# A twentieth buffer for weights in a two-block transformer kernel, and ten pairs of buffers from the ninth expert on

## The chip, the core and the metric

The kernel runs as one launch on one core of one Trainium2 chip. The metric is the device time of an execution in microseconds (us). Three runs of the kernel before took 1641.13, 1641.85 and 1643.40 us; their median, 1641.85 us, is the time before. The execution that was profiled took 1642.62 us, and its instructions span 1640.8 us.

## The reference

Two transformer blocks work on 256 tokens of width 1024, all in float32. The first has a mixer (sliding-window attention beside gated linear attention) and then a mixture of 32 experts, of which each token takes four. The second is a dense block with two feed-forward layers around another mixer. What matters here is the mixture:

```python
logits = (h @ w_router) + b_router
top_v, top_i = lax.top_k(logits, 4); gates = jax.nn.softmax(top_v, axis=-1)
...
u = xb @ w_mlp1[e] + b_mlp1[e]                 # w_mlp1[e]: 1024 x 2048, 8 MB
a = x_glu * jax.nn.sigmoid(1.702 * x_glu) * (x_lin + 1)   # x_glu, x_lin clipped at 7
y = a @ w_mlp2[e] + b_mlp2[e]                  # w_mlp2[e]: 1024 x 1024, 4 MB
out = zeros.at[slot_tok].add(y * gate)
x = x + gt2 * rms_norm(out, g_post_ffn)
```

Every expert's 12 MB are read once, so the mixture reads 384 MB, and the whole program 547 MB.

## The kernel before

**Slots.** Weights go from the chip's memory through buffers of 8192 bytes a partition, 1 MB each, called slots (`SLOT`, `NSLOT = 19`). Slots 0 to 6 (`NEAR = 7`) belong to the weights all the time. Slots 7 to 18 ("far" in the code) lie over tiles of the first mixer, and each may be filled only when its gate (`slot_gate`, L1162 to L1167, L1276 and L1303) is open, which means that the tiles under it have had their last reader. Behind slot 18 begins the region (`moe0`, L234) with `gg2` (the row with which the mixture's output is scaled at its end), `brow`, the split weights `whf`/`wlf` of the mixer, and the small tiles of the mixture.

**Chunks.** I number the 1 MB chunks of the mixture 0 to 383: chunk 12e + j is the j-th of expert e, j = 0 to 7 of `w_mlp1` and 8 to 11 of `w_mlp2`. They are loaded in that order, all by SyncE's queue (SP in the profile), which is one list made at L2119 to L2134: each load waits until the chunk that held its slot has been read for the last time, and a load that waits holds back all behind it. TensorE gives the sign: behind the last matmul of every chunk it raises the semaphore `rel`. I call this the release of the chunk.

**Which slot.** For experts 0 to 8 (`LONE = 9`) every load is one chunk, and the slots follow the list `order` of 19 numbers, again and again (L298 to L301). For experts 9 to 30 one load brings two chunks (2 MB) into a pair of neighbouring slots. The pairs follow `ring` (L303), which has nine of them, starting at slots 7, 9, 11, 13, 15, 17, 1, 3 and 5; slot 0 is not used then. A pair's load waits for the releases of both chunks that lie in its two slots. The list of pairs is cut at its front (L304), so that it ends with the ring's end at expert 30. Expert 31 has single loads again, in slots 7 to 18. The dense block that follows uses slots 0 to 6 alone.

**Experts.** The program has for each expert three ways: for up to 32 tokens (near), up to 64 (middle), and more (far, L1638), and each engine branches by the count. TensorE, VectorE and ScalarE pass the chunk's results on in the usual way: first matmuls with `w_mlp1`, then the gated activation (DVE, ACT), transposes, and second matmuls with `w_mlp2`. Between the first and the second an odd expert also gathers the tokens of the next two experts (`prepare`).

**gg2.** It is written by ScalarE's queue early, before expert 0 (L1713): two loads of 256 KB, each of 128 rows of 2 KB. It is read by `residual` after expert 31 (L1764).

Of the kernel before, what the change touches and what calls it, by code (L numbers as in the profile page):

```python
# [7 lines left out]
F32 = mybir.dt.float32  # L8
F32R = mybir.dt.float32r
# [4 lines left out]
D = 1024  # L14
NE = 32
EPS = 1e-6
SLOT = 8192
NEAR = 7
NSLOT = 19
LONE = 9  # L20
NPIECE = 4
NEG = -1.0e30
FAR = 3.0e38
# [131 lines left out]
def two_block_forward(  # L155
# [31 lines left out]
    with ctx:  # L187
# [7 lines left out]
        end = nc.sbuf_usable_end // 32 * 32  # L195

        place = {}

        class Arena:
# [30 lines left out]
        z0 = near + NEAR * SLOT  # L230
        slots = [
            nc.alloc_sbuf_tensor_at(f"slot{i}", [128, 2048], F32, offset=near + i * SLOT) for i in range(NSLOT)
        ]
        moe0 = near + NSLOT * SLOT  # L234
        both = {
            i: nc.alloc_sbuf_tensor_at(f"slots{i}", [128, 4096], F32, offset=near + i * SLOT)
            for i in [*range(NEAR, NSLOT, 2), 1, 3, 5]
        }


        slot_sem = [sem(f"slot{i}") for i in range(NSLOT)]
        chunks = []
        slot_gate = [[] for _ in range(NSLOT)]

        def chunk(src, slot, width=2048):
            chunks.append({"src": src, "slot": slot, "sem": slot, "w": width, "done": None})
            return len(chunks) - 1

        def two_chunks(src, slot):

            first = chunk(src, slot, 4096)
            chunks.append({"src": None, "slot": slot + 1, "sem": slot, "w": 2048, "done": None})
            return [first, first + 1]
# [42 lines left out]
        c_out = stream(lambda j: w_out[j], 4, slots_=(0, 1, 4, 2))  # L296

        far = lambda *i: [NEAR + j for j in i]  # L298
        order = [3, 5] + far(1) + [6] + far(0) + [0] + far(3, 6, 7) + [1] + far(5, 2) + [4] + far(4) + [2] + far(9, 10, 11, 8)
        assert sorted(order) == list(range(NSLOT))  # L300
        singles = order * NE  # L301
        last_singles = far(*range(12))
        ring = [*range(NEAR, NSLOT, 2), 1, 3, 5]  # L303
        pairs = (ring * NE)[-6 * (NE - 1 - LONE) :]  # L304
        c_w1, c_w2 = [], []
        for e in range(NE):
            if LONE <= e < NE - 1:
                ids = [two_chunks(w[e, j], pairs.pop(0)) for w, n in ((w_mlp1, 4), (w_mlp2, 2)) for j in range(n)]
                ids = [i for two in ids for i in two]
            else:  # L310
                src = [w[e, j // 2][:, j % 2 * 2048 : j % 2 * 2048 + 2048] for w, n in ((w_mlp1, 8), (w_mlp2, 4)) for j in range(n)]
                ids = [chunk(i, singles[12 * e + j] if e < LONE else last_singles[j]) for j, i in enumerate(src)]
            c_w1.append(ids[:8])
# [42 lines left out]
        def load(q, s, dst, src, *after):  # L356
# [35 lines left out]
        bias_ada = [nc.alloc_sbuf_tensor_at("badat0", [128, 512], F32, offset=place["gg"][0]), badat]  # L392
        wl_last = rare("wl_last", [128, 1024], F32R)
# [11 lines left out]
        og = over("og", "att_s0", "att_s0", [128, 2, 512])  # L405
        atth1 = over("atth1", "gq", "gat", [128, 4, 256], F32R)
        attl1 = over("attl1", "gqt", "gkt", [128, 4, 256], F32R)
        later = Arena(moe0, end)
        gg2 = later("gg2", [128, D])
        bias_ada.append(nc.alloc_sbuf_tensor_at("badat2", [128, 512], F32, offset=place["gg2"][0]))  # L410
        brow = later("brow", [128, 1536], F32R)
        rare = Arena(z0 + 10 * SLOT, moe0)
        XH = rare("XH", [128, 8, 256], F32R)
        XL = rare("XL", [128, 8, 256], F32R)
        sq = over("sq", "XH", "XH", [128, D])
        tmp2 = over("tmp2", "XL", "XL", [128, 2, D])
        np_slots = [
            (later(f"whf{i}", [128, 1024], F32R), later(f"wlf{i}", [128, 1024], F32R) if i < NPIECE - 1 else wl_last)
            for i in range(NPIECE)
        ]  # L420
        wrt = later("wrt", [128, 8, NE])
        tri_s = later("tri_s", [128, 128])

# [4 lines left out]
        s_gg, s_gg2 = sem("s_gg"), sem("s_gg2")  # L428
# [74 lines left out]
        pieces = []  # L503
# [52 lines left out]
        T = {}  # L556
# [41 lines left out]
        def rows_in(dst, r0, s_, *after):  # L598
            return [load(act, s_, dst[:, 512 * g : 512 * g + 512], mod_rows[r0 + g : r0 + g + 1, :].to_broadcast([128, 512]),
                         *after) for g in range(2)][-1]  # L600
# [28 lines left out]
        p_out = add_pieces(c_out)  # L629
# [32 lines left out]
        for k in range(8):  # L662
            i = k % 4
            src = bank[2 + i][:, (k // 4) * 256 : (k // 4) * 256 + 256]
            a_, b_ = a1[:, k : k + 1], sh1[:, k : k + 1]
# [495 lines left out]

        for i, gate_ in enumerate((  # L1162
            [T["pv"]], [T["pt1"]], [T["ov"], T["o"]], [T["pv"], T["o"]], [pieces[p_out + 3]["used"]], [t_og], [T["o"], T["r"]],
            [T["o"], T["r"]], [], [], [], [],
        )):
            slot_gate[NEAR + i] = gate_

# [3 lines left out]
        moe = Arena(place["brow"][1], end)  # L1171
# [7 lines left out]
        u_g, u_s, u_l = (moe(n, [128, 512]) for n in ("u_g", "u_s", "u_l"))  # L1179
# [10 lines left out]
        xt_x = moe("xt_x", [128, 8, 32])  # L1190
        at_x = nc.alloc_sbuf_tensor_at("at_x", [128, 4, 64], F32, offset=place["xt_x"][0])
        sel32 = [[moe(f"sel32{i}{j}", [128, 64]) for j in range(2)] for i in range(2)]
        y_x = moe("y_x", [64, D])


        t_tr, t_ns = [[], []], []
# [32 lines left out]
        def selections(p):  # L1229

            i = p % 2
            pool.wait([pe.now()])
            for s_ in range(2):
                e = 2 * p + s_
                one = zsel[:, :].rearrange("p (h e) -> p h e", h=2)[:, :, e : e + 1]
                cp(pool, sel32[i][s_][:, :].rearrange("p (h j) -> p h j", h=2), one.to_broadcast([128, 2, 32]))
                t_selt[i] = cp(pool, selt[i][s_][:, :].rearrange("p (h j) -> p h j", h=2), one.to_broadcast([128, 2, 64]))
# [112 lines left out]
        def prepare(p, half):  # L1350
            i = p % 2
            ks = range(4 * half, 4 * half + 4)
            if p == 0:
                new = gather(oh, xt, t_oh[0], ks=ks, b0=2, at=slice(64, 128))
                t_xt[0] = [t_xt[0][0], (t_xt[0][1] if half else []) + new]
                if half:
                    t_ws[0], _ = weights_t(ow, ws[0], 3, t_ow[0])
                return
            new = gather(oh, xt, t_oh[i], ks=ks)
            t_xt[i] = [t_xt[i][s_] + new for s_ in range(2)] if half else [new, new]  # L1360
            if half:
                t_ws[i], _ = weights_t(ow, ws[i], 1, t_ow[i])
# [347 lines left out]
            q.wait([t_a2, t_sh2])  # L1710
        t_xt[0] = [gather(oh, xt, t_first[0], b0=2, at=slice(0, 64)), []]

        T["gg2"] = rows_in(gg2, 2, s_gg2, T["gg2"])  # L1713
        t_nm = ts(dve, nmax, top8[:, :, 0], -1.0, ALU.mult, t_sl1)
        for b in range(2):
            t_e = af(gate[:, b, :], lg[:, b, :], ACT.Exp, t_nm, bias=nmax[:, b : b + 1])
# [10 lines left out]
        for p in range(NE // 2):  # L1727
            if 0 < p < NE // 2 - 1:
                one_hots(p + 1)
                selections(p + 1)  # L1730
            t_even = expert(2 * p, [lambda b=b: scatter(p - 1, False, [b]) if p else prepare(0, b) for b in range(2)])
            if p == 0:
                one_hots(1)
                selections(1)
            t_odd = expert(2 * p + 1, [lambda h_=h_: prepare(p + 1, h_) for h_ in range(2)] if p + 1 < NE // 2 else [nothing] * 2)
            t_yp[p % 2] = t_even + t_odd
        warm(3, 0)
# [324 lines left out]
        for b in range(2):  # L2062
            for g in range(2):
                c = slice(512 * g, 512 * g + 512)
# [172 lines left out]
```

How the kernel before makes its waits and increments, by code:

```python
    def run(items):  # L69
        for it in items:
            if it[0] == "wait":
                eng.wait_ge(it[1], it[2])
            elif it[0] == "op":
                it[1](eng)
            elif it[0] == "sig":
                it[1](eng).then_inc(it[2], it[3])
            elif it[0] == "step":
                eng.sem_inc(it[1], it[2])
            elif it[0] == "home":
```

## Time and profile before

| what | us |
|---|---|
| median of 3 runs | 1641.85 |
| lowest and highest run | 1641.13, 1643.40 |
| profiled execution | 1642.62 |
| its span | 1640.8 |
| TensorE busy in the span | 1445.6 (88%) |
| VectorE, ScalarE, GpSimd busy | 589.1, 471.4, 123.0 |
| experts 0 to 31, first to last matmul, about | 160 to 1085 |
| dense block after them | 1085 to 1640 |

The profile is of one execution. In its strip of 40 slices a slice is 41 us. "DMA" is the mean busy share of the 16 DMA engines over which each transfer is spread; a transfer has landed when all its parts have, so its landing tells of the last engine. In the views of windows the columns are the window's ends, its length, the busy time of each engine with its count of instructions, the granted clock of TensorE, the DMA share and the rate.

### The profile page before, as it was taken

The page shows a single profiled execution, that of the slowest core. Times are in us where ns is not written, and L with a number is a line of the kernel's source. Part 1 is how long each engine was busy: PE and PEld are TensorE (multiplying, and loading weights), DVE is VectorE, ACT ScalarE, POOL GpSimd, SP SyncE. Part 2 cuts the span into 40 slices and gives each one's busy share as a digit, 9 for nine tenths or more (in the row PEclk, how much of TensorE's full clock was granted, in tenths as well). Part 3 has the DMA queues.
Part 4 walks back from the last instruction along what each step waited for, and adds up shares of the span by engine and source line. Part 5 has one row for each costly group of instructions (what it writes and reads, how often), then busy time and mean ns, then how long its engine had stood idle before and what let it go on. Part 6 is the DMA issues. An engine that isn't in the chain of part 4 may idle for free.

```text
span 1640.8 us, 20608 instructions
## 1 busy us (share of the span) xinstructions
PE 1445.6 (88%) x8414; PEld 842.7 (51%) x8414; DVE 589.1 (36%) x957; ACT 471.4 (29%) x836; POOL 123.0 (7%) x254
## 2 busy tenths in 40 slices
PE   5999988896868787887689788899999999999998
PEld 2767433332322332332233233258888878788886
DVE  3676211220110111221111111156654677665654
ACT  3644201110110110110000101045553674565543
POOL 2001301110110110110110110000000010000000
PEclk9999989998889997999889999999999999999999
DMA  9999999999999999989999999986555443555540
GB/s 384 404 359 361 420 423 425 424 424 429 429 429 428 429 427 429 397 339 430 429 426 428 428 428 428 426 346 224 181 200 184 180 133 124 230 195 203 178 157 26
DMA packets 57944, 547.43 MB, mean 334 GB/s; under 512 B 6548, under 2 KB 6932, under 8 KB 9000
## 3 DMA queue, kind: packets, MB, share of 16 engines
q1 hardware_dynamic: 56736, 542.95, 80.8%
q8 instruction: 107, 1.75, 0.4%
q10 hardware_dynamic: 1032, 2.16, 0.4%
q14 instruction: 69, 0.57, 0.1%
HBM read 544.03 MB, written 1.06 MB: 332 GB/s over the span
## 4 chain that ended last, share of the span: by engine, by line
PE 64%; DMA 25%; issue 4%; DVE 3%; POOL 2%; ACT 1%; POOLq 0%; DVEq 0%; SPq 0%; ACTq 0%
PE bank L330 62%; DMA slots<-w_mlp 20%; DMA slot<-w_mlp 4%; PE bank L334 2%; DMA slot<-w_in_tail 1%; POOL oh L345 1%; POOL ow L345 1%; DVE u_l L348 0%; DVE u_l L345 0%; DVE u_g L344 0%; DVE u_s L340 0%; PE bank L1472 0%; DVE h L348 0%; DVE XL L340 0%; ACT xt L337 0%
## 5 line engine op out<-in xcount | busy, mean ns | idle before, releaser
L330 PE MATMUL bank<-slots,xt 128*32 128x512 f32 (+1 forms) x1408 | 268.6, 702 | 67.2 <-DMA slots<-w_mlp 66.4
L330 PE MATMUL bank<-wht,XH 128*128 128x512 f32 x528 | 207.1, 397 | 4.4 <-DVE wlt L340 2.7
L348 DVE SCALAR_TENSOR_TENSOR wlt<-slot,colt,wht 128x512 fp32r<-128x512 f32 x248 | 177.4, 761 | 79.2 <-ACT wht L337 79.0
L344 DVE TENSOR_SCALAR u_g<-bank 64x512 f32<-64x512 f32 (+1 forms) x34 | 23.3, 686 | 503.3 <-PE bank L330 496.0
L330 PE MATMUL bank<-wht,XL 128*128 128x512 f32 x528 | 203.7, 390 | 0.0
L330 PE MATMUL bank<-wlt,XH 128*128 128x512 f32 x528 | 203.6, 390 | 0.0
L330 PEld LDWEIGHTS bank<-slots,xt 128*32 128x32 f32 (+1 forms) x1408 | 71.6, 135 | 256.2 <-issue 152.4
L337 ACT ACTIVATE wht<-slot,colt 128x512 fp32r<-128x512 f32 x248 | 164.5, 718 | 92.3 <-PE bank L330 92.3
L337 ACT ACTIVATE u_s<-u_g 64x512 f32<-64x512 f32 (+1 forms) x34 | 21.4, 630 | 525.7 <-DVE u_g L344 525.7
L330 PE MATMUL bank<-slots,at 128*32 128x256 f32 (+1 forms) x1120 | 112.8, 436 | 4.6 <-DMA slots<-w_mlp 3.1
L330 PEld LDWEIGHTS bank<-wht,XH 128*128 128x128 f32 x528 | 99.0, 188 | 26.5 <-issue 3.9
L330 PE MATMUL bank<-slot,xt 128*32 128x512 f32 (+1 forms) x640 | 102.3, 628 | 10.1 <-DMA slot<-w_mlp 10.0
L330 PEld LDWEIGHTS bank<-wht,XL 128*128 128x128 f32 x528 | 99.2, 188 | 21.2
L330 PEld LDWEIGHTS bank<-wlt,XH 128*128 128x128 f32 x528 | 99.3, 188 | 19.4
L340 DVE TENSOR_TENSOR wlt<-slot,wht 128x1024 fp32r<-128x1024 f32 x60 | 73.4, 1225 | 68.2 <-ACT wht L337 68.0
L345 POOL TENSOR_SCALAR oh<-iota,pos,stat 128x64 f32<-128x64 f32 x60 | 34.6, 577 | 719.7 <-PE bank L334 719.7
L337 ACT ACTIVATE wht<-slot 128x1024 fp32r<-128x1024 f32 x60 | 63.5, 1061 | 77.2 <-PE bank L330 77.2
L330 PEld LDWEIGHTS bank<-slots,at 128*32 128x32 f32 (+1 forms) x1120 | 45.1, 117 | 68.3 <-issue 47.8
L330 PEld LDWEIGHTS bank<-oh,h 128*128 128x128 f32 x544 | 63.2, 192 | 16.7 <-issue 15.7
L330 PEld LDWEIGHTS bank<-slot,xt 128*32 128x32 f32 (+1 forms) x640 | 27.6, 123 | 82.5 <-issue 58.6
L330 PE MATMUL bank<-brow,selt 128*128 128x512 f32 x36 | 19.9, 617 | 56.3 <-issue 56.0
L330 PE MATMUL bank<-oh,h 128*128 128x128 f32 (+1 forms) x544 | 68.7, 280 | 0.2 <-DVE oh L345 0.2
(329 smaller groups left out, 1670.9 us busy)
## 6 DMA issues: line engine op xcount, KB each, us to landing
slots<-w_mlp SPq DMA_DIRECT2D x132, 2048.0 KB, 39.2
slot<-w_mlp SPq DMA_DIRECT2D x120, 1024.0 KB, 25.0
slot<-gu SPq DMA_DIRECT2D x44, 1024.0 KB, 4.8
slot<-w_ada SPq DMA_DIRECT2D x24, 1024.0 KB, 10.2
slot<-down SPq DMA_DIRECT2D x22, 1024.0 KB, 4.8
slot<-w_in SPq DMA_DIRECT2D x18, 1024.0 KB, 5.7
slot<-w_out SPq DMA_DIRECT2D x8, 1024.0 KB, 9.2
slot<-w_gate SPq DMA_DIRECT2D x8, 1024.0 KB, 4.8
```

Of the source, the lines that this page charges most:

```text
L330: return pe(lambda e: e.matmul(o, l, r, start=start, stop=stop), *after, **kw)
L334: return pe(lambda e: e.transpose(o, i, ident[:, :]), *after, **kw)
L337: return act(lambda e: e.activation(o, i, func, **kw), *after)
L340: return q(lambda e: e.tensor_tensor(o, a, b, op), *after)
L344: return q(lambda e: e.tensor_scalar(o, a, s1, None, op0=op0), *after)
L345: return q(lambda e: e.tensor_scalar(o, a, s1, s2, op0=op0, op1=op1), *after)
L348: return dve(lambda e: e.scalar_tensor_tensor(o, a, s, b, op0, op1), *after)
```

## The change

`NSLOT` becomes 20: a slot 19 is put behind slot 18, over the mixer's `whf0` and `wlf0` and over `gg2`, which are moved there. Its gate for the first load is the last use of `whf0`/`wlf0` in the output projection. `order` gets 20 numbers, with slot 19 (`far(12)`) ahead of slot 16. `LONE` becomes 8: the ninth expert, number 8, already uses pairs. The ring has ten pairs, starting at slots 6, 8, ..., 18, 0, 2 and 4. `gg2` is loaded between experts 30 and 31 in place of before expert 0, when the last chunk in slot 19 has been released. The far way's `y_x` lies over `u_s` now, and `badat2` has a place of its own.

```diff
-NSLOT = 19
-LONE = 9
+NSLOT = 20
+LONE = 8
...
-            for i in [*range(NEAR, NSLOT, 2), 1, 3, 5]
+            for i in range(0, NSLOT, 2)
...
-        order = [3, 5] + far(1) + [6] + far(0) + [0] + far(3, 6, 7) + [1] + far(5, 2) + [4] + far(4) + [2] + far(9, 10, 11, 8)
+        order = [3, 5] + far(1) + [6] + far(0) + [0] + far(3, 6, 7) + [1] + far(5, 2) + [4] + far(4) + [2] + far(12, 9, 10, 11, 8)
...
-        ring = [*range(NEAR, NSLOT, 2), 1, 3, 5]
+        ring = [*range(NEAR - 1, NSLOT, 2), *range(0, NEAR - 1, 2)]
...
+        top = Arena(z0 + 12 * SLOT, moe0)
+        gg2 = nc.alloc_sbuf_tensor_at("gg2", [128, D], F32, offset=top.lo + 2048)
         later = Arena(moe0, end)
-        gg2 = later("gg2", [128, D])
-        bias_ada.append(nc.alloc_sbuf_tensor_at("badat2", [128, 512], F32, offset=place["gg2"][0]))
...
+        np_slots = []
+        for i in range(NPIECE):
+            a_ = later if i else top
+            hi = a_(f"whf{i}", [128, 1024], F32R)
+            np_slots.append((hi, a_(f"wlf{i}", [128, 1024], F32R) if i < NPIECE - 1 else wl_last))
+        bias_ada.append(later("badat2", [128, 512]))
...
-            [T["o"], T["r"]], [], [], [], [],
+            [T["o"], T["r"]], [], [], [], [], [pieces[p_out + 7 - (p_out + 7) % NPIECE]["used"]],
...
-        y_x = moe("y_x", [64, D])
+        y_x = nc.alloc_sbuf_tensor_at("y_x", [64, D], F32, offset=place["u_s"][0])
...
-        T["gg2"] = rows_in(gg2, 2, s_gg2, T["gg2"])
...
+            if p == NE // 2 - 1:
+                T["gg2"] = rows_in(gg2, 2, s_gg2, T["gg2"], [c for c in chunks if c["slot"] == NSLOT - 1][-1]["done"])
```

**Where the single loads end.** This is SyncE's list at the place where pairs begin, before. A name is the slot's number and a running number of the buffer; `slots13` is the pair of slots 13 and 14. "waits rel" is a wait for a release; a row without it needs nothing that was not waited for already.

```order
L357 DMA slot13_80<-w_mlp1 128x2048 [waits rel]
L357 DMA slot14_81<-w_mlp1 128x2048 [waits rel]
L357 DMA slot1_68<-w_mlp2 128x2048 [waits rel]
L357 DMA slot12_79<-w_mlp2 128x2048 [waits rel]
L357 DMA slot9_76<-w_mlp2 128x2048 [waits rel]
L357 DMA slot4_71<-w_mlp2 128x2048 [waits rel]
L357 DMA slots13_89<-w_mlp1 128x4096 [waits rel]
L357 DMA slots15_90<-w_mlp1 128x4096
L357 DMA slots17_91<-w_mlp1 128x4096
L357 DMA slots1_92<-w_mlp1 128x4096 [waits rel]
```

The first pair takes slots 13 and 14, filled six and five chunks ahead of it (chunks 102 and 103). The same place now:

```order
L357 DMA slot4_71<-w_mlp2 128x2048 [waits rel]
L357 DMA slot11_78<-w_mlp2 128x2048 [waits rel]
L357 DMA slot2_69<-w_mlp2 128x2048 [waits rel]
L357 DMA slot19_86<-w_mlp2 128x2048 [waits rel]
L357 DMA slots10_92<-w_mlp1 128x4096 [waits rel]
L357 DMA slots12_93<-w_mlp1 128x4096
L357 DMA slots14_94<-w_mlp1 128x4096
L357 DMA slots16_95<-w_mlp1 128x4096
L357 DMA slots18_96<-w_mlp2 128x4096 [waits rel]
L357 DMA slots0_87<-w_mlp2 128x4096
```

The first pair takes slots 10 and 11 now. Slot 11 was filled three chunks ahead of it, with chunk 93, the second `w_mlp2` chunk of expert 7; between it and the pair stand slot 2 (chunk 94) and slot 19 (chunk 95) alone.

**The first load of slot 19.** SyncE's list where expert 1's chunks are loaded for the first time, now:

```order
L357 DMA slot11_78<-w_mlp1 128x2048 [waits pe]
L357 DMA slot2_69<-w_mlp1 128x2048 [waits dve]
L357 DMA slot19_86<-w_mlp1 128x2048 [waits pe]
L357 DMA slot16_83<-w_mlp1 128x2048 [waits dve]
L357 DMA slot17_84<-w_mlp1 128x2048
```

The row of slot 19 is new and stands ahead of slot 16, which waits for the last write of `h`.

## Rows read from the trace of the kernel before

**Rows 1.** The page's strip: 40 slices of 41 us, tenths and GB/s.

```profile
PEclk9999989998889997999889999999999999999999
DMA  9999999999999999989999999986555443555540
GB/s 384 404 359 361 420 423 425 424 424 429 429 429 428 429 427 429 397 339 430 429 426 428 428 428 428 426 346 224 181 200 184 180 133 124 230 195 203 178 157 26
```

**Rows 2.** Windows: the long stretches in which experts run.

```profile
160.00:360.00 200.00, 179.38 (x1342) 77.40 (x1345) 41.41 (x90) 29.90 (x70) 23.50 (x53) 0.95 1.01 423
360.00:700.00 340.00, 261.39 (x1671) 98.39 (x1664) 49.96 (x100) 31.21 (x73) 31.70 (x72) 0.89 1.00 423
715.00:1071.00 356.00, 291.13 (x1872) 111.13 (x1870) 50.79 (x93) 32.83 (x75) 26.48 (x60) 0.92 1.01 428
```

**Rows 3.** Chain that ended last, in order: start us, us, what.

```profile
363.32 26.52 DMA slot<-w_mlp
...
1036.34 34.92 DMA slot<-w_mlp
...
1077.40 7.84 PE bank L330 x35
...
1087.36 0.70 ACT sqr L337 x2
```

**Rows 4.** Timeline of SyncE's queue: issues, start us, us. Narrow windows.

```profile
139.34 0.33 SPq L357 DMA_DIRECT2D slot<-w_mlp  x1
152.23 0.33 SPq L357 DMA_DIRECT2D slot<-w_mlp  x1
329.95 4.92 SPq L357 DMA_DIRECT2D slot<-w_mlp  x1
688.50 0.33 SPq L357 DMA_DIRECT2D slots<-w_mlp  x1
705.78 0.33 SPq L357 DMA_DIRECT2D slots<-w_mlp  x1
```

**Rows 5.** DMA issues in the same five windows, last column us to landing.

```profile
slot<-w_mlp SPq DMA_DIRECT2D x1, 1024.0 KB, 11.4
slot<-w_mlp SPq DMA_DIRECT2D x1, 1024.0 KB, 5.2
slot<-w_mlp SPq DMA_DIRECT2D x1, 1024.0 KB, 29.7
slots<-w_mlp SPq DMA_DIRECT2D x1, 2048.0 KB, 18.0
slots<-w_mlp SPq DMA_DIRECT2D x1, 2048.0 KB, 7.7
```

**Rows 6.** Timeline of TensorE, experts 7 and 8 (brackets: idle before, and releaser).

```profile
359.75 3.66 PE L330 MATMUL bank<-slot,at 128*32 128x256 f32 x64
...
365.46 0.16 PEld L330 LDWEIGHTS bank<-slot,xt 128*32 128x32 f32 x8 [0.95 <-DMA slot<-w_mlp]
367.88 0.16 PEld L330 LDWEIGHTS bank<-slot,xt 128*32 128x32 f32 x8 [2.26 <-DMA slot<-w_mlp]
370.31 0.20 PEld L330 LDWEIGHTS bank<-slot,xt 128*32 128x32 f32 x8 [2.27 <-DMA slot<-w_mlp]
```

**Rows 7.** Windows at the two idle places of the DMA engines.

```profile
150.00:152.00 2.00, 2.00 (x17) 1.65 (x15) 1.89 (x4) 1.28 (x3) 0.54 (x1) 1.00 0.06 16
...
696.00:700.00 4.00, 0.00 (x0) 0.00 (x0) 0.00 (x0) 0.00 (x0) 0.00 (x0) 0.75 0.69 285
700.00:704.00 4.00, 3.19 (x12) 0.69 (x15) 0.00 (x0) 0.00 (x0) 0.00 (x0) 0.50 0.08 29
```

**Rows 8.** Timeline of TensorE, between experts 17 and 18.

```profile
690.52 3.70 PE L330 MATMUL bank<-y_x,ws_x 64*128 64x512 f32 x8
700.81 1.97 PE L330 MATMUL bank<-brow,sel 128*64 128x512 f32 x4 [6.59 <-issue]
702.72 8.09 PE L330 MATMUL bank<-slots,xt 128*32 128x512 f32 x64
```

**Rows 9.** DMA queues: packets, MB, share of 16 engines; windows 160:168, 360:700, 360:360.2.

```profile
q10 hardware_dynamic: 288, 0.52, 17.0%
...
q8 instruction: 26, 0.43, 0.5%
q14 instruction: 19, 0.16, 0.1%
...
q14 instruction: 1, 0.01, 9.7%
```

**Rows 10.** Timeline of ScalarE, between experts 30 and 31.

```profile
1054.07 0.76 ACT L1496 ACTIVATE ypair<-bank 32x256 f32<-32x256 f32 x2 [5.15 <-PE bank L330]
1073.15 0.63 ACT L337 ACTIVATE u_s<-u_g 128x512 f32<-128x512 f32 x1 [18.32 <-DVE u_g L344]
```

More of the change, by code:

```diff
@@ L416, in two_block_forward @@
         tmp2 = over("tmp2", "XL", "XL", [128, 2, D])
[L417 to L420, printed above, removed]
+        np_slots = []
[4 more added lines that the diff above has]
+        bias_ada.append(later("badat2", [128, 512]))
+        later = Arena(end - 4096, end)
         wrt = later("wrt", [128, 8, NE])
```

## The prediction

> **What bounds the kernel now.** I read the strip of slices first. The DMA row is full and the rate 420 to 430 GB/s from the fifth slice to the end of the mixture, with a dip in the 17th and 18th slice (397 and 339 GB/s, about 656 to 738 us); behind 1100 us the rate falls to half and TensorE is the one that is busy [rows 1]. Windows say the same in numbers: DMA share 1.01, 1.00 and 1.01 in three stretches that cover 160 to 1071 us [rows 2]. The chain of waits names the link between the two parts: the load issued at 1036.34 lands at 1071.26, and TensorE's last matmuls of expert 31 follow to 1085.24 [rows 3]. So what is before 1071.26 is set by the stream of weights, and a change there counts only if it moves the landing of chunk 379 (expert 31's last of w_mlp1). The 570 us behind it are the same work on the same seven slots, and I shift them as they are.
>
> More buffers carry no byte faster. They can only close places at which the stream stands still because SyncE waits for a release. I looked for these places by windows and found two.
>
> At 150 us: the share is 0.06 from 150 to 152 [rows 7]. The load issued at 139.34 lands at 150.7 and the next is issued at 152.23, when the last gate of the mixer opens, and lands at 157.4 [rows 4, 5]. Two landings 1 MB apart are 2.42 or 2.43 us apart in a full stream (365.46, 367.88, 370.31) [rows 6]; here they are 6.7 apart, a loss of 4.3.
>
> At 700 us: experts 17 (a far one) and 18 are slower on TensorE than their weights arrive, all slots are full, and the share falls to 0.69 and 0.08 [rows 7]. What it costs is not the idle share. A share of 0.08 is a little over one engine of sixteen (0.06): one engine still works off its part while the others wait. The load issued at 688.50 lands at 706.5, the one issued at 705.78 at 713.5 [rows 4, 5]. These landings are 7.0 us apart where 4.85 (two times 2.43) is the distance in a full stream. The engine that is last therefore lost only 2.1 us, though the mean share of the dip looks like ten. I call it the slow engine. It is behind because instruction fetches come between the weights: 26 and 19 packets in 360 to 700 us [rows 9].
>
> **The first load of slot 19: about 0.** One more MB can be loaded ahead of the gate at 152.23, which would cover 2.43 of the 4.3 us. It counts at the end only if the stream then runs without another stop of its own, and the next part puts in one which is timed by TensorE. TensorE itself is behind the stream until expert 7 (in 160 to 360 it is busy 179 of 200 us [rows 2]), and does not start sooner. So: 0; bounds -2.4 (no such stop) and 0.
>
> **The new handover from single slots to pairs: +4.0.** Before, the first pair waits for chunk 103, five ahead of it. Now the first pair (chunks 96 and 97) goes to slots 10 and 11 and waits for chunk 93, three ahead of it; behind it stands the whole stream. Chunk 93 is the second of four w_mlp2 chunks of expert 7. Their 64 matmuls run from 359.75 for 3.66 us, 16 for each chunk [rows 6], so chunk 93 is released at 359.75 + 1.83 = 361.6. This time is TensorE's own and stays. But the load issued at 329.95, chunk 95, has landed by 359.65 [rows 4, 5], and with one more slot it lands 2.4 sooner. So the queue is empty, all 16 engines stand still, and the stream starts anew at 361.6. Such a start has a row: issued at 705.78 with all but one engine idle, 2 MB landed 7.7 us later [rows 4, 5]. Chunk 97 lands at 361.6 + 0.1 + 7.7 = 369.4. Before, it landed by 365.46, where TensorE waits for it [rows 6]. Difference 4.0 us. The four next pairs are released by 363.4, so nothing else waits. From here to expert 17 the stream is full before and after, and TensorE is again and again at its heels (the chain waits for the landing at 389.84 [rows 3]), so both move by 4.0. Six pair loads in place of twelve single ones in expert 8 give perhaps 0.1. Bounds: 3.0 (start as after the gate, 5.2 for 1 MB, plus 2.43, less 0.7 if the slow engine is among the first to land) and 5.0 (the fetches near 364 come to the engine that is last).
>
> The Trainium skill, in "DMA: Bandwidth & Descriptors", Anatomy of one DMA — SWDGE (gpsimd) path, fits a transfer as about 2.0 us and its bytes by 436 GB/s. That makes 6.8 us of a 2 MB load, and the sum would be 0.9 less, 2.3 in place of 3.2. The row has 7.7 on SyncE's queue and I stay with it.
>
> **Ten pairs in the ring: -2.1.** Before, a pair waits for the pair nine before it; now for the one ten before it. The load at 688.50 was released by the end of expert 17's second matmuls, the one at 705.78 by the first chunks of expert 18, between them the scatter, a wait of 6.59 us for instructions and matmuls at half clock (0.50) [rows 7, 8]. Now the load that was issued at 705.78 goes out with the earlier release, at about 688.5 + 4.0, and the next at 705.8 + 4.0 = 709.8, while the slow engine works until 706.5 + 4.0 + 4.85 = 715.4 on what it has. With 2 us to start it is 3 us in time. The whole 2.1 is gone, the other engines still pause, and the slow one keeps its lag. What is late next is again the stream: it goes on full to chunk 379. Bounds: 0 (the next rival but one) and -4 (below).
>
> **gg2: +1.3.** Two loads of 256 KB in rows of 2 KB. Before, they ran in 160 to 168 us: 17.0% of 16 engines in 8 us, 1.36 us of each [rows 9], ahead of the new stop, where they no longer count. Now they are issued behind ScalarE's last work for expert 30, at about 1055 [rows 10], while the stream is full and chunk 379 lands 16 us later. If the engines take them in between, every later landing moves by 1.36. Bounds: 0, if they run behind what is queued, and 1.4. TensorE doesn't wait for them: they are read at about 1087 [rows 3]. The row at 160 shows them taken between weights at once, though with few weights queued, and I take 1.3. The Trainium skill, same page, Queues, rings and completion order, says that each DMA engine goes round its queues packet by packet; by it the 1.3 stands with a full queue too, and no row here shows that case.
>
> The moves of y_x, badat2, whf0 and wlf0 change addresses alone: 0. ScalarE issues the two loads between experts, where it is idle for 18 us [rows 10].
>
> **Sum.** 0 + 4.0 - 0.1 - 2.1 + 1.3 = +3.1. The profiled execution takes 1642.62 us (span 1640.8 and 1.8 around it) and becomes 1645.7; it stands 0.77 above the median, so the median becomes 1645.0. That is 0.19% more. About 0.2%, or 3.3 us, is what a measurement of this kernel can tell from no change.
>
> **Rivals.**
> 1. It works as it says: the handover makes no stop, because chunk 93 is released before the queue is empty. For it: the handover before left no mark, the share stays at 1.01 across 381. Against it: that one waited for a chunk on which TensorE was at the stream's heels, and here chunk 95 has landed 2 us before the release even with 19 slots. Time: -2.4 at the gate, -2.1 at 705, +1.3 for gg2 (its early cost falls in an idle place): 1638.7.
> 2. The slow engine is another after 705. Before, all engines start level at 705.78; the lag that grows to 1071 may be one engine's that was not last before 705. That one pauses until 709.8 and lands 2 MB at 709.8 + 7.7 = 717.5; before it landed them at 713.5 + 4.85 = 718.3. Then its end is -0.8 + 1.3 = +0.5, so 1642.4. Against it: the fetches of branches at other times seem to hit one engine (a single engine busy in 700 to 704 [rows 7] after 340 us of fetches, of which an even spread would leave a small lag), and nothing suggests it changes.
> 3. Slower: the stop at 705 returns. The margin there is 3 us. The stretch holds a wait for instructions of 6.59 us [rows 8] and matmuls at half clock; if that stretch gets 3 us longer against the stream, or a start needs 5 us and not 2, the two new slots give nothing at this place and the handover is paid in full: 4.0 - 0.1 + 1.3 = +5.2, 1647.0. It decides from a release of chunk 217 later than about 712.8. For it: these waits vary with how instructions lie. Against it: no step of the change is in that stretch.
>
> **How the numbers follow.** My forecast 0.60 (its own range 1643.7 to 1646.3, with both sides of +0.2% at 1645.1 nearly alike, 0.28 slower and 0.32 within), rival 1 0.12, rival 2 0.14, rival 3 0.14 (slower but for 0.01). Slower by over 0.2%: 0.28 + 0.13 = 0.41; within 0.2%: 0.32 + 0.14 + 0.01 = 0.47; faster: 0.12. The range reaches from below rival 2, towards rival 1, to above rival 3: 1640.5 to 1647.5.
>
> **What would show it.** In the profile after: a window near 358 to 363 us with a DMA share near 0, SyncE's issue of the first pair at 361.6 to 361.8, its landing near 369.4; around 705 to 712 no distance of landings above 4.9 us but single engines busy; two small loads on ScalarE's queue near 1060; chunk 379 landing at 1074.4, and the dense block of 570 us unchanged. Wrong if the share stays at 1 around 360 (rival 1), if chunk 379 lands by 1072 though the stop at 360 is there (rival 2 or gg2 behind the queue), or if landings near 712 are 7 us apart (rival 3).

## The result, and the profile after

The changed kernel takes 1645.74 us (median of 10 runs, 1644.03 to 1651.16), the kernel before 1642.51 (10 runs, 1641.13 to 1646.89): the ratio is 1.0023, with a 95% interval from 1.0013 to 1.0033. The forecast was 1645.0, with a range from 1640.5 to 1647.5. A second series gave 1645.82 (11 runs) against 1643.09, 1.0019 [1.0008, 1.0030].

The first profile of the changed kernel is of an execution that took 1650.34 us, 4.6 above its median. TensorE's granted clock was 0.50 of full, its lower level of 1.2 GHz, while it gathered the rows of expert 0, and this took 6.93 us where it takes 3.76 at full clock. The first row is TensorE's timeline in that execution, the second the same work in the second series' profiled execution of the same kernel (1645.82 us).

```profile
158.59 6.93 PE L330 MATMUL bank<-oh,h 128*128 128x64 f32 x32 [0.22 <-DVE oh L345]
```

```profile
157.69 3.76 PE L330 MATMUL bank<-oh,h 128*128 128x64 f32 x32 [0.37 <-DVE oh L345]
```

So I read the changed kernel in the second execution, and the first only to see what such a delay does. The strip of the page, 40 slices of 41.1 us, of the second:

```profile
PEclk9999989997989997999899988999999999999999
DMA  9999999979999999999999999976455433555440
GB/s 383 406 362 378 417 423 424 425 323 429 429 429 429 430 427 428 431 394 430 429 426 428 425 431 428 426 314 231 180 192 193 179 131 126 226 198 200 179 158 26
```

Against [rows 1] there is one new hole, the ninth slice (424 to 323 GB/s, 329 to 370 us). The old one has become smaller: 397 and 339 before, 431 and 394 now. Windows around the new hole (us from start to end, busy time of PE, PEld, DVE, ACT and POOL, granted clock, DMA share, GB/s):

```profile
354.00:358.00 4.00, 3.63 (x33) 2.48 (x25) 2.71 (x4) 2.02 (x5) 0.00 (x0) 1.00 0.17 66
358.00:362.00 4.00, 4.00 (x54) 3.13 (x58) 1.37 (x4) 0.77 (x3) 1.73 (x4) 1.00 0.00 0
362.00:366.00 4.00, 2.77 (x40) 0.98 (x28) 0.85 (x2) 0.74 (x2) 3.57 (x9) 1.00 0.73 225
```

The last completion of chunk 95 comes at 356.93 and the next load is issued at 362.15, so all sixteen DMA engines stand still for five us while TensorE is busy. The chain of waits in the same place says for what. TensorE's 32 matmuls on chunks 92 and 93 end, and SyncE issues the load of the first pair:

```profile
359.95 0.22 PE bank L334 x2
360.17 1.91 PE bank L330 x32
...
362.15 0.33 SPq L357
```

The DMA issues in a window of 0.5 us around this load (last column: us to landing), and TensorE's timeline, where the first matmuls of expert 8 wait for it:

```profile
slots<-w_mlp SPq DMA_DIRECT2D x1, 2048.0 KB, 8.2
```

```profile
360.10 3.66 PE L330 MATMUL bank<-slot,at 128*32 128x256 f32 x64
363.69 1.08 PE L330 MATMUL bank<-brow,sel 128*64 128x512 f32 x4
370.36 1.94 PE L330 MATMUL bank<-slots,xt 128*32 128x512 f32 x8 [5.59 <-DMA slots<-w_mlp]
```

Chunk 97 lands at 362.15 + 8.2 = 370.3. In [rows 6] the wait for it ended at 365.46: 4.9 later.

The second place is the one of [rows 4, 5 and 7]. Windows of the changed kernel there:

```profile
696.00:700.00 4.00, 2.56 (x6) 0.75 (x5) 0.00 (x0) 0.00 (x0) 3.71 (x10) 1.00 1.02 438
700.00:704.00 4.00, 0.00 (x1) 0.00 (x0) 0.00 (x0) 0.00 (x0) 0.00 (x0) 0.69 1.01 424
704.00:708.00 4.00, 3.90 (x15) 0.88 (x18) 0.00 (x0) 0.00 (x0) 0.00 (x0) 0.50 0.65 279
```

The share falls only after 704, and its lowest in any microsecond of 704 to 713 is 0.34 (709 to 710), never one engine in sixteen. SyncE's timeline has the load of chunks 234 and 235, which went out at 705.78 before, and the one behind it. They are 17 us apart, as the loads issued at 688.50 and 705.78 were:

```profile
692.22 0.33 SPq L357 DMA_DIRECT2D slots<-w_mlp  x1
...
709.18 2.04 SPq L357 DMA_DIRECT2D slots<-w_mlp  x2
```

The landings of chunks 233 and 235 are at 709.75 and 714.61, 4.86 apart, where they were 6.91 apart (706.54, 713.45). (Here and below a landing is the last of the 16 completions of a load.)

The third place is behind expert 30. TensorE's timeline on the first chunks of expert 31, where each group of 8 matmuls waits for its chunk:

```profile
1058.41 1.94 PE L330 MATMUL bank<-slot,xt 128*64 128x512 f32 x8 [0.39 <-DMA slot<-w_mlp]
1061.23 1.94 PE L330 MATMUL bank<-slot,xt 128*64 128x512 f32 x8 [0.89 <-DMA slot<-w_mlp]
1064.31 1.94 PE L330 MATMUL bank<-slot,xt 128*64 128x512 f32 x8 [1.14 <-DMA slot<-w_mlp]
1067.03 1.94 PE L330 MATMUL bank<-slot,xt 128*64 128x512 f32 x8 [0.79 <-DMA slot<-w_mlp]
1069.48 1.94 PE L330 MATMUL bank<-slot,xt 128*64 128x512 f32 x8 [0.51 <-DMA slot<-w_mlp]
```

The distances are 2.82, 3.08, 2.72 and then 2.45 us. Three chunks carry 1.27 us more than a full stream gives them. ScalarE's timeline has the cause, 2 us before, and the DMA queues in 1050 to 1074 us show the same 288 packets on q10 as [rows 9]:

```profile
1055.57 0.35 ACTq L357 DMA_DIRECT2D gg<-mod_rows  x1
...
1055.95 0.45 ACTq L357 DMA_DIRECT2D gg<-mod_rows  x1
```

```profile
q10 hardware_dynamic: 288, 0.52, 5.7%
```

The chain at the end of the stream, to set beside [rows 3]:

```profile
1043.85 30.48 DMA slot<-w_mlp
...
1080.47 7.84 PE bank L330 x35
...
1090.43 0.70 ACT sqr L337 x2
```

Chunk 379 lands at 1043.85 + 30.48 = 1074.33 where it was 1071.26, +3.07. From there to the end of the span it is 569.67 us, and was 569.54.

Five landings, by kernel, show where it went. They are in us, each from the one profiled execution of its kernel; "after" is the second execution, and e1, e6, e9 and e10 are experiments described below:

| chunk | before | after | e1 | e6 | e10 | e9 |
|---|---|---|---|---|---|---|
| 97 | 365.42 | 370.32 | 362.67 | 362.82 | 368.91 | 362.95 |
| 233 | 706.54 | 709.75 | 703.46 | 703.31 | 708.00 | 703.63 |
| 235 | 713.45 | 714.61 | 708.31 | 708.17 | 712.85 | 708.49 |
| 371 | 1051.70 | 1053.51 | 1047.50 | 1047.10 | 1051.76 | 1047.41 |
| 379 | 1071.26 | 1074.33 | 1068.33 | 1067.93 | 1071.30 | 1066.95 |

### The profile page after: what moved, and what is told of

Read it like the earlier page. It is cut to its first block, busy times and chain, and to the rows that moved or that the text cites. A ratio compares the mean times of both kernels' runs of the same rounds, so it can differ in the third digit from the quotient of the medians.

```text
span 1648.5 us, 20602 instructions
## 1 busy us (share of the span) xinstructions
PE 1447.3 (88%) x8409; PEld 845.6 (51%) x8414; DVE 589.2 (36%) x957; ACT 471.5 (29%) x836; POOL 123.5 (7%) x254
## 4 chain that ended last, share of the span: by engine, by line
PE 64%; DMA 26%; DVE 4%; issue 3%; POOL 2%; ACT 1%; SPq 0%; POOLq 0%; DVEq 0%; ACTq 0%
PE bank L330 61%; DMA slots<-w_mlp 23%; PE bank L334 2%; DMA slot<-w_mlp 2%; DMA slot<-w_in_tail 1%; DVE u_l L348 1%; DVE u_l L345 1%; DVE u_g L344 1%; DVE u_s L340 1%; POOL oh L345 1%; POOL ow L345 1%; PE bank L1475 0%; DVE h L348 0%; DVE XL L340 0%; SPq L357 0%
## 5 line engine op out<-in xcount | busy, mean ns | idle before, releaser
L330 PE MATMUL bank<-slots,xt 128*32 128x512 f32 (+1 forms) x1472 | 277.4, 701 | 77.2 <-DMA slots<-w_mlp 76.5
L330 PE MATMUL bank<-slots,at 128*32 128x256 f32 (+1 forms) x1184 | 116.5, 433 | 4.7 <-DMA slots<-w_mlp 3.2
L330 PE MATMUL bank<-slot,xt 128*32 128x512 f32 (+1 forms) x576 | 92.2, 623 | 4.7 <-DMA slot<-w_mlp 4.7
L330 PEld LDWEIGHTS bank<-oh,h 128*128 128x128 f32 x544 | 66.7, 200 | 16.3 <-issue 15.8
L330 PE MATMUL bank<-ypair,ws 128*128 128x512 f32 x128 | 62.9, 615 | 0.1
```

The source lines that it names most:

```text
L330: return pe(lambda e: e.matmul(o, l, r, start=start, stop=stop), *after, **kw)
```

## The experiments

The experiments ran in three series (e1 to e4, e5 to e8, e9 and e10). The medians of the kernel before in them are 1642.89, 1643.09 and 1643.29; each ratio is to the runs of the kernel before in the same series.

**e1: twenty slots, pairs from the tenth expert on as before.** The changed kernel with

```
-LONE = 8
+LONE = 9
```

> Twenty slots as in the changed kernel, but pairs from the tenth expert on, as before; the first pair then takes slots 2 and 3 and waits for chunk 100, eight chunks ahead of it. My theory (the stream stops at the handover because the first pair waits for a chunk that TensorE has not released): no stop near 360 us, the 2.4 us of the gate at 152 us and the 2.1 us of the stop at 705 us are kept, gg2 costs 1.3: about -3.1 us against before, ratio 0.998, and the first pair's load goes out while several loads are queued. Rival (the handover is innocent; what the change costs is the late load of gg2 and new addresses): still 2 to 3 us slower than before, ratio 1.0015 to 1.002.

Measured: 1641.78 us (11 runs), ratio 0.9994 [0.9983, 1.0004]. A window of this kernel at the place of the stop:

```profile
358.00:362.00 4.00, 4.00 (x50) 3.22 (x54) 1.36 (x4) 1.19 (x4) 1.31 (x3) 1.00 1.01 422
```

There is no stop. Chunk 97 lands 2.75 earlier than before: this is the start slot 19 gives, and it is kept. Chunks 233 and 235 are 4.85 apart; chunk 379 is 2.93 earlier, and so is the span by 2.84. The median fell by 1.1 only: the interval reaches past 1 and leaves out the 0.998 that I expected. The profiled execution, 1639.79, is the fastest of the eleven. The mechanism is shown by the trace, the size at the median is less than expected. The rival (1.0015 to 1.002, the handover is innocent) is outside the interval.

**e2: the kernel before with gg2 loaded late.**

```
-        T["gg2"] = rows_in(gg2, 2, s_gg2, T["gg2"])
...
+            if p == NE // 2 - 1:
+                T["gg2"] = rows_in(gg2, 2, s_gg2, T["gg2"])
```

> The kernel before, with the two loads of gg2 alone moved between experts 30 and 31. My theory (the DMA engines take them between the weights that are queued): the landings of expert 31's chunks have one step that is 1.3 us too long in sum, chunk 379 lands 1.3 us later, less some 0.3 us that the early load no longer takes: +1.0 us, ratio 1.0006. Rival (they run behind what is queued, or beside it): 0 or -0.3 us, ratio 1.000, and no step in the landings.

Measured: 1645.74 us (6 runs), 1.0026 [1.0013, 1.0039]. The chunks after 371 come as they should: TensorE's timeline has 1059.07, 1062.14 and 1065.08, distances of 3.07 and 2.94, and chunk 379 lands 1.14 later, near the 1.0 that I expected. But the time of 1.0006 that I expected is outside the interval, and the span of the profiled execution is 2.77 longer. The other 1.6 us are in the dense block, 350 us later, where TensorE's clock fell once more. A window of this kernel, and the same of the kernel before:

```profile
1428.00:1432.00 4.00, 4.00 (x17) 3.37 (x16) 0.89 (x2) 1.17 (x3) 0.00 (x0) 0.62 0.72 262
```

```profile
1428.00:1432.00 4.00, 4.00 (x23) 3.39 (x22) 2.52 (x3) 2.50 (x4) 0.00 (x0) 1.00 0.53 223
```

The granted clock is 0.62 of full here, where it is 1.00 in the kernel before. Why it fell is open. The profiled executions of e7, e9 and e10 have such a stretch too, those of the other kernels don't. Whether the other runs of e2 have it no trace shows.

**e3 and e4: TensorE starts the experts late,** in the kernel before and in the changed one. 27 matmuls on a tile of zeros more, ahead of the first gather (6.21 us for 28 of them in the trace):

```
-        add_nothing(1)
+        add_nothing(28)
```

> The kernel before, with 27 more matmuls that add zeros ahead of expert 0, so that TensorE enters the experts about 5.8 us later. My theory (before, the stream doesn't wait for TensorE until 705 us, and TensorE has caught up with it by then): the 5.8 us vanish, ratio 1.000 to 1.0005. Rival (a late start of TensorE is simply added to the end): +5.8 us, ratio 1.0035.

> The changed kernel with the same 27 matmuls ahead of expert 0. My theory (the handover ties the stream to TensorE's release of chunk 93): the first pair goes out 5.8 us later and so does everything behind it: +5.8 us on the changed kernel, which is +9.0 us on the kernel before, ratio 1.0055. Rival (the delay is hidden as in the kernel before, so that the slow executions of the changed kernel have another cause): about +3.2 us, ratio 1.002.

Measured: e3 1649.03 us (5 runs), 1.0035 [1.0021, 1.0048]; e4 1653.98 (5 runs), 1.0062 [1.0049, 1.0076]. My theory for e3 was that TensorE has room before 360 us and only the stream counts. It fell, and the rival's 1.0035 is what was measured. Windows of e3, and of the kernel before:

```profile
163.00:165.00 2.00, 2.00 (x16) 1.62 (x15) 0.00 (x0) 0.00 (x0) 0.00 (x0) 1.00 0.62 262
165.00:167.00 2.00, 2.00 (x20) 2.00 (x20) 0.00 (x0) 1.23 (x4) 0.00 (x0) 1.00 0.05 19
```

```profile
163.00:165.00 2.00, 2.00 (x24) 0.65 (x20) 1.00 (x5) 1.71 (x3) 0.13 (x1) 1.00 0.97 389
165.00:167.00 2.00, 2.00 (x24) 0.52 (x16) 0.00 (x0) 0.11 (x1) 2.00 (x4) 1.00 1.05 344
```

The load of chunk 19 waits for the release of chunk 0. Even in the kernel before this comes a little late: the load is issued at 163.82, and chunks 18 and 19 land 3.96 us apart (165.17, 169.13) where a full stream has 2.43. The share of the window, 0.97, hides it. What TensorE loses ahead of expert 0 is lost by the stream at 165 us (chunk 20 lands 5.9 later), and comes out at the end. In the profiled execution of e3 chunk 97 lands 6.1 later and chunk 379 8.3: the stop at 705, which TensorE times too, is 1.3 longer, and the rest comes behind it.

In the changed kernel the load of chunk 20 waits for chunk 0, and the handover waits for TensorE again. The expected 1.0055 of e4 is inside its interval and the rival's 1.002 outside. In its profiled execution chunk 97 lands 8.3 later than in the undelayed one, more than the 5.8 that was put in: TensorE released chunk 0 at 170.98 in place of 163.49, and its clock was at half for 3.4 us from 156.5 on, which it was not in the undelayed one.

**e5: the changed kernel once more.**

> The changed kernel as it is, once more, because its first profile began TensorE's part 6 us late. Theory: without that delay chunk 93 is released near 361.6 to 362.5 us, the load of chunks 96 and 97 is issued right behind it and lands 7.7 to 8.5 us later (near 369.4 to 370.5), chunk 379 lands near 1074.3 and the time is 1.0019 to 1.0023 of the kernel before. Rival: the late start is part of the change (buffers at other places in front of the experts); then this profile too has TensorE 5 to 6 us late at 165 us and chunk 379 lands at 1078 to 1079.

Measured: 1645.82 us (11 runs), 1.0019 [1.0008, 1.0030]. It is the execution shown above: the clock was full at 157 us, chunk 97 landed at 370.3 and chunk 379 at 1074.3, as expected. TensorE began expert 0 at 162.38, so the rival (the late start is part of the change) falls.

**e6: the changed kernel with other first pairs.**

```
-        last_singles = far(*range(12))
-        ring = [*range(NEAR - 1, NSLOT, 2), *range(0, NEAR - 1, 2)]
-        pairs = (ring * NE)[-6 * (NE - 1 - LONE) :]
+        last_singles = [2, 3, 16, 17, 6, 7, 14, 15, 18, 12, 13, 11]
+        ring = [16, 6, 14, 0, 12, 8, 4, 10, 2, 18]
+        pairs = (ring * NE)[: 6 * (NE - 1 - LONE)]
```

> The changed kernel with nothing but other numbers in the ring: the pairs take the slots in the order 16, 6, 14, 0, 12, 8, 4, 10, 2, 18, so that the first pair waits for chunk 77 (nineteen ahead) and every later one for a chunk at least eleven ahead; the last expert's chunks go to slots 2, 3, 16, 17, 6, 7, 14, 15, 18, 12, 13, 11. Twenty slots, pairs from the ninth expert on and the late load of gg2 stay. Theory (the stop at the handover is the price): no window with an empty queue near 360 us, chunk 97 lands near 363, chunk 379 near 1068.3 as in the kernel with pairs from the tenth expert on, time 0.998 to 0.9995 of the kernel before. Rival (pairs in the ninth expert cost something by themselves, or slot 19's load does): chunk 379 lands at 1074 and the time is 1.002.

Measured: 1640.73 us (11 runs), 0.9983 [0.9971, 0.9995]. Windows of it at the handover, and the chain's load that ends with chunk 379:

```profile
354.00:358.00 4.00, 3.63 (x31) 2.29 (x24) 2.71 (x4) 1.76 (x5) 0.00 (x0) 1.00 1.04 434
358.00:362.00 4.00, 4.00 (x54) 3.16 (x56) 1.37 (x4) 1.04 (x4) 1.46 (x3) 1.00 0.99 420
```

```profile
1037.46 30.47 DMA slot<-w_mlp
```

Only slot numbers differ from the changed kernel: those of the pairs and those of the last expert's chunks. TensorE does its 64 matmuls of expert 7 at 360.37, as late as there, and the stream does not notice. Chunk 97 lands 7.5 us earlier than after, chunk 379 6.4 earlier, the median is 5.1 lower. This is the price of the stop. The rival's 1.002 is outside the interval, and chunk 379 lands 6 us ahead of the rival's 1074.

**e7: e1 with gg2 loaded in the stream itself,** and **e10: the same edit in the changed kernel**; **e9: in e6.**

```
-                T["gg2"] = rows_in(gg2, 2, s_gg2, T["gg2"], ...)
+                extras[c_w2[NE - 1][3]] = [
+                    (s_gg3, gg2[:, 512 * g : 512 * g + 512],
+                     mod_rows[2 + g : 3 + g, :].to_broadcast([128, 512]), [T["gg2"], free19])
+                    for g in range(2)
+                ]
```

> Twenty slots with pairs from the tenth expert on, and gg2's two loads issued by SyncE in the stream itself, behind chunk 383 (the last of the experts' weights), in place of ScalarE between experts 30 and 31. Theory (the late load costs 1.3 us because the engines take it in between weights that TensorE waits for): the landings of chunks 371 and 379 are 19.5 to 19.6 us apart in place of 20.8, chunk 379 lands near 1067.0, and the time is 1.1 to 1.4 us under that of the kernel with pairs from the tenth expert on: near 1640.5, 0.9985. Rival (the bytes have to be loaded anyway, and the 1.3 us comes back behind chunk 383, before the dense block): chunk 379 lands at 1067.0 but the span behind it is 1.3 us longer, and the time stays near 1641.8.

> The changed kernel with gg2's two loads in the stream behind chunk 383 and nothing else: the handover with its stop stays. Theory (the sum of the prediction: 4.0 for the handover, -2.1 for the tenth pair, 1.3 for gg2): 1.3 us less than the changed kernel, chunk 379 near 1073.0, time 1.0010 to 1.0014 of the kernel before. Rival (gg2 costs more than its bytes, as the +2.9 us of the kernel before with gg2 loaded late and the 2.0 us gained with pairs from the tenth expert on could be read): 2 to 3 us less, 1.0000 to 1.0005.

> The changed kernel with both costs taken out: pairs from the ninth expert on in the order 16, 6, 14, 0, 12, 8, 4, 10, 2, 18, and gg2's two loads issued by SyncE in the stream behind chunk 383. Theory (the two costs are separate and add): chunk 379 lands 1.3 us before that of the kernel with the other first pairs, near 1066.6, and the time is 1639.4, 0.9975 of the kernel before. Rival (with gg2 out of the way the wait for TensorE's releases or for the stream takes over, so that only one of the two gains counts): chunk 379 near 1067.9 and 0.9983.

Measured: e7 1639.81 us (12 runs), 0.9979 [0.9969, 0.9990]; e10 1644.78 (12 runs), 1.0014 [1.0004, 1.0024]; e9 1639.62 (12 runs), 0.9974 [0.9962, 0.9985]. TensorE's timeline of e7 in expert 31:

```profile
1055.33 1.94 PE L330 MATMUL bank<-slot,xt 128*64 128x512 f32 x8 [0.49 <-DMA slot<-w_mlp]
1057.76 1.94 PE L330 MATMUL bank<-slot,xt 128*64 128x512 f32 x8 [0.49 <-DMA slot<-w_mlp]
1060.23 1.94 PE L330 MATMUL bank<-slot,xt 128*64 128x512 f32 x8 [0.54 <-DMA slot<-w_mlp]
```

The distances are 2.43 and 2.47, with no slower chunk. Chunks 371 and 379 are 19.56 apart in e7, 19.54 in e9 and e10, 19.56 before, against 20.82 after. The same bytes cost 1.3 us between the weights and none behind them. At the median the edit gave 2.0 us (e7 against e1), 1.0 (e10 against the changed kernel) and 1.1 (e9 against e6). In each of the three pairs the two intervals overlap, so the 1.3 rests on the landings, and the medians only agree with it.

Two rivals are named above that the times can't exclude: e10's upper end of 1.0005 and e9's 0.9983 are inside the intervals. The landings speak against both (19.54 between chunks 371 and 379 in e10, chunk 379 at 1066.95 in e9, where that rival has 1067.9). Two of my numbers were off. In e7 chunk 371 came 0.5 later than in e1, so chunk 379 gained 0.76. In e10 chunk 379 landed at 1071.3, not 1073.0: TensorE's clock fell once less before 360 us (it released chunk 80 at 339.89, in the changed kernel at 341.60), so the handover, which is timed by TensorE, was 1.7 earlier.

All three profiled executions then lost about 1.5 in the dense block, as e2 did. This looks like e7's rival, by which the 1.3 us come back behind chunk 379, but its place is another: to 318 us behind chunk 379 VectorE's instructions come at the same distance from it as in e1, the changed kernel and the kernel before, within 0.1 us, and the 1.5 come between 319 and 406 us behind it, where the stretch at half clock is (from 1422 us on in e7). So the rival's cause is not there. What these three executions don't show is a shorter span: e7's is 1638.6, e1's 1638.0.

e9 is faster than both kernels: by 3.7 us than the kernel before in its own series, and by 6.1 than the changed kernel, across series. That it beats e6 and e7 is not shown: their intervals overlap.

**e8: nineteen slots, pairs from the ninth expert on.** The kernel before with

```
-LONE = 9
+LONE = 8
```

> The kernel before with one number changed, pairs from the ninth expert on: nineteen slots, nine pairs, gg2 loaded early. The pair of chunks 98 and 99 then waits for chunk 95, three ahead of it, with the pair 96 and 97 still queued before it. Theory (what a stop costs is the distance of two landings of the engine that is last): this pair is issued near 363.5, the slow engine is busy with chunk 97 until 365.4, and chunk 99 lands 7.7 us after the issue, near 371.2, in place of 370.3: +0.9, which stays to the end; the stop at 705 is there as before; time +0.9, 1.0005. Rival (a handover three chunks ahead costs 4 us with any number of slots): 1.0024.

Measured: 1643.53 us (11 runs), 0.9997 [0.9984, 1.0010]. The rival's 1.0024 is outside; whether it costs 0 or 0.9 is not told apart. Windows of it:

```profile
358.00:362.00 4.00, 3.63 (x32) 2.92 (x30) 1.43 (x4) 1.81 (x6) 0.00 (x0) 1.00 1.00 430
362.00:366.00 4.00, 4.00 (x68) 2.18 (x68) 1.53 (x5) 0.56 (x2) 3.73 (x7) 1.00 0.23 92
```

The stop is there, but it is short: the last completion of chunk 97 comes at 366.14, after the next pair has been issued. The pair 98 and 99 is issued at 365.8 and lands 7.7 us later, as long as expected. But in this profiled execution TensorE was 2.3 late (its 64 matmuls of expert 7 began at 362.10, before at 359.75), after a longer stretch at half clock near 274 us (10.2 us, before 6.8) and 3.4 us more each near 230 and 319, and chunk 379 landed 3.1 later. The median is within 0.5 us of the kernel before's and has no such loss.

## Why the prediction was right, point by point

The prediction was right in its mechanism: the new stop, what times it, the place of the second gain and the price of `gg2` are each shown by a trace. e1 and e6 take away the stop, and e7, e9 and e10 the price of `gg2`. That the total fits to 0.1 us is luck in part, as the terms show. They are from the landings in the table:

- **The first load of slot 19: 0, with a bound of -2.4 if no other stop follows.** Right on both sides. After: the gain ends in the stop. With the stop taken away (e1, e6) chunk 97 lands 2.75 and 2.60 earlier than before.
- **The handover: +4.0 and -0.1.** The mechanism is shown, by the chain and by e6. The size at chunk 97 was 4.9. The release came at 362.1 in place of 361.6, since TensorE was 0.35 later, and the load took 8.2 us from issue to landing, not 7.7. The 0.1 for six pair loads had no row behind it; from chunk 97 to 107 the stream was 0.07 faster. Of the 4.9, 3.2 were left at chunk 233. I had no step for the 1.7 that came back. 1.4 of it lies between chunks 107 and 143, and it goes with the stop: the last of the sixteen completions needs 113.9 to 114.9 us from chunk 97 to 143 in the four profiled executions of twenty slots that have the stop, and 115.3 to 115.6 in the kernel before, e1, e6, e7 and e9, which don't. Why is not settled. The number of 8 KB instruction fetches between these chunks is the same (four before, four after).
- **Ten pairs: -2.1.** From 6.91 to 4.86 us between chunks 233 and 235: -2.05. The load went out at 692.2 and the next at 709.18 (forecast 709.8), while the slow engine was still at work; its completion for that next load is 2.4 us behind all others. The two landings are as close in e1 and e6. No run has twenty slots and nine pairs, so the tenth pair is not tried by itself. And the old distance varies: in the other profiled executions with nineteen slots it is 6.04 (e2), 8.24 (e3) and 7.14 (e8), so what ten pairs gain lies between 1.2 and 3.4 us, and the 2.1 is the value of the one execution that I read. The prediction's reason for the slow engine, instruction fetches, has a trace behind it: before, the last completion is 0.94 us behind the one ahead of it at chunk 109 and 1.90 at chunk 111, 1.82 at chunk 117 and 2.84 at chunk 119, and an 8 KB fetch begins in between each time (395.0, 419.6).
- **gg2: +1.3.** +1.26 between chunks 371 and 379, and 1.27 in the distances of TensorE's waits. e7, e9 and e10 take it away by putting the same loads behind the weights. So what no row of before could show is shown: with a full queue on SyncE, ScalarE's small loads are taken in between at once. That agrees with what the Trainium skill says in "DMA: Bandwidth & Descriptors", Queues, rings and completion order: each DMA engine goes round its queues packet by packet. The prediction's other estimate from that page (6.8 us for 2 MB, by the fit in Anatomy of one DMA — SWDGE (gpsimd) path) is from a fit for GpSimd's path, and is too low for SyncE's queue here: the start from an empty queue took 8.2 and 8.6 us in the two profiled executions of the changed kernel. (The sum it was set against is 3.1, not the 3.2 that stands there, so by that estimate it would have been 2.2.)
- From chunk 235 to 371 the changed kernel lost 0.65 more, for which I had no step either. This is no cost of the change: the profiled execution of the kernel before needs 338.25 us there, and the three others with nineteen slots 338.76 to 338.94 (e2, e3, e8), against 338.90 after.
- Together 4.9 - 1.7 - 2.05 + 0.65 + 1.26 = 3.06, the forecast's 3.1. The sum is this good because two misses, +0.9 at the handover and -1.0 behind it (-1.7 and 0.65, with the 0.1 that was forecast), nearly cancel. At the median the change costs 3.2 us in the first series and 2.7 in the second.

**The rivals.** 1 (no stop) is excluded for the changed kernel. Its sum, -3.2, is near what chunk 379 of e6 shows (-3.33), where the stop is taken away; at the median e6 gained 2.4. 2 (another slow engine after 705) would have chunk 379 at +0.5, it was +3.07. 3 (the stop at 705 returns) needed a release after 712.8, it was at 709.2. In all eight profiled executions with twenty slots chunks 233 and 235 are 4.85 to 4.87 apart.

**A step that was wrong, without a price here.** The prediction found two places at which the stream stands still, and none between 160 and 360 us. The landings of chunks 18 and 19 show a third, at 165 us, where the stream waits for TensorE already in the kernel before. It changed no term, because the change does not move TensorE's start, but it hid a cost: what TensorE loses ahead of expert 0 comes out at the end (e3), and in the changed kernel what it loses between there and 360 us does so too, through the handover. The first profile of the changed kernel is such a case. TensorE began the matmuls of expert 0 at 167.35 us in place of 162.38, and at half clock, and chunk 379 landed at 1078.97, 4.6 after that of the second; windows of the first execution at both places:

```profile
165.00:170.00 5.00, 5.00 (x23) 1.31 (x26) 2.18 (x10) 1.82 (x3) 1.37 (x3) 0.50 0.00 0
...
362.00:366.00 4.00, 4.00 (x50) 3.17 (x54) 1.37 (x4) 1.14 (x4) 1.35 (x3) 1.00 0.02 10
```

## What to carry to other kernels

- When a ring of buffers is laid out anew, write down for every load how many loads ahead of it the one stands whose release it needs. The smallest number, at the handover from one layout to the other, shows where the stream may stop. Three ahead, with nothing else left in the queue, cost 6.4 us at chunk 379 and 5.1 at the median; the same slots in another order made no stop. The number alone does not decide: in e8 a pair also waits for a chunk three ahead, and its median shows no loss.
- A small load that is needed late belongs in the stream, behind the last bytes that something waits for. On a queue of its own it was served at once here, and pushed those bytes back by 1.26 us, about its own time (1.36).
- Gains and stops don't add up by idle shares but by landings: compare the last of the sixteen completions of the same chunk in both traces.

## What the runs showed of the hardware

- A start from an empty queue costs more than the idle time: 2 MB issued with all engines idle landed after 8.2 and 8.6 us in the changed kernel (7.8 in e4, 8.5 in e10), where two chunks in a full stream are 4.85 apart.
- The sixteen DMA engines drift apart in a full stream. In the kernel before the first completion of the load of chunks 198 and 199 is 14.5 us ahead of its last.
- TensorE's granted clock differs between executions of one kernel, and a stop that TensorE times carries this to the end. In the first profile of the changed kernel the clock was at half (1.2 GHz) for 13.7 us from 156.4 us on, and chunk 379 landed 4.6 us later than in the second. e10 has one short stretch at half clock less (3.4 us, near 230 us), and its handover was 1.7 earlier.
- In the dense block one more stretch at half clock, near 1425 us, made the part behind chunk 379 last 571.0 to 571.2 us, in place of 569.5 to 569.7, in four of the twelve profiled executions. What decides it is open.
